# Mixing wide and narrow expert passes unit by unit in a two-block hybrid layer on one Trainium2 core

## The reference

```
def swiglu(x, w_gate, w_up, w_down):
    return (jax.nn.silu(x @ w_gate) * (x @ w_up)) @ w_down

def moe_swiglu(x, router_w, w_gate, w_up, w_down):
    logits = (x @ router_w).astype(jnp.float32)
    top_v, top_i = lax.top_k(logits, TOP_K)            # TOP_K = 2
    gates = jax.nn.softmax(top_v, axis=-1)
    combine = jnp.sum(jax.nn.one_hot(top_i, N_EXPERTS, dtype=jnp.float32) * gates[..., None], axis=-2)
    y = jnp.zeros_like(x)
    for e in range(N_EXPERTS):                         # 8 experts, inner width 3584
        y = y + combine[..., e:e + 1].astype(x.dtype) * swiglu(x, w_gate[e], w_up[e], w_down[e])
    return y
```

## Time and profile before

| | |
|---|---|
| median of three runs | 2535.86 us (2533.59 to 2536.7) |
| the profiled execution, its own time | 2543.58 us |
| its span | 2541.5 us |
| busy in the span: PE, DVE, ACT | 96%, 74%, 56% |
| HBM read | 589.79 MB, 232 GB/s over the span |
| expert passes written out, first split to last | 1590.4 to 2381.5 us of the span |
| the looped pass | 2393.1 to 2513.5 us |

### The profile page before, as it was taken

How to read it: one execution, slowest core, us unless ns; L and a number is a source line. 1 busy time by engine, 2 the same in 40 slices (tenths; PEclk the granted TensorE clock), 3 DMA queues, 4 the chain that set the end, 5 groups by cost and what they waited for, 6 DMA issues and landing times.

```text
span 2541.5 us, 36256 instructions
## 1 busy us (share of the span) xinstructions
PE 2433.5 (96%) x14462; PEld 2103.4 (83%) x14462; DVE 1880.7 (74%) x2198; ACT 1424.2 (56%) x1578; POOL 0.2 (0%) x4
## 2 busy tenths in 40 slices
PE   7999999999999999989999998999999999999897
PEld 7999989899998998886997885787777777888786
DVE  7665755567657543986554985889999999988787
ACT  4654444456545343423342422678888888777574
POOL 0000000000000000000000000000000000000000
PEclk9999999999999999999999998999999999999998
DMA  6333464343345444304534302899999999999796
GB/s 253 138 119 133 154 244 183 149 146 145 117 162 203 178 188 165 134 36 166 199 150 155 145 3 100 337 360 404 412 412 413 413 413 412 382 347 367 287 354 261
DMA packets 119623, 593.19 MB, mean 233 GB/s; under 512 B 17440, under 2 KB 17824, under 8 KB 77472
## 3 DMA queue, kind: packets, MB, share of 16 engines
q1 hardware_dynamic: 110224, 585.40, 59.8%
q10 hardware_dynamic: 9232, 5.47, 0.8%
HBM read 589.79 MB, written 1.05 MB: 232 GB/s over the span
## 4 chain that ended last, share of the span: by engine, by line
PE 69%; DVE 18%; DMA 5%; issue 4%; ACT 3%; DVEq 0%; SPq 0%; ACTq 0%; POOLq 0%
PE bank L608 21%; PE bank L2512 17%; PE bank L865 12%; DVE wlo L687 6%; DMA ring<-in_stream 5%; PE bank L1717 4%; DVE ring_lo L839 2%; ACT whi L682 2%; PE bank L1133 2%; DVE big L2967 1%; PE bank L1148 1%; PE bank L1738 1%; PE bank L1903 1%; PE bank L2452 1%; DVE big L2141 1%
## 5 line engine op out<-in xcount | busy, mean ns | idle before, releaser
L687 DVE TENSOR_TENSOR wlo<-ring,whi 128x2048 fp32r<-128x2048 f32 x430 | 979.0, 2289 | 113.0 <-ACT whi L682 108.8
L682 ACT ACTIVATE whi<-ring 128x2048 fp32r<-128x2048 f32 x433 | 825.9, 1912 | 111.6 <-PE bank L2512 51.4
L2512 PE MATMUL bank<-whi,xhi 128*128 128x512 f32 x896 | 367.7, 410 | 16.3 <-DVE wlo L687 12.5
L2512 PE MATMUL bank<-wlo,xhi 128*128 128x512 f32 x896 | 353.0, 394 | 0.0
L839 DVE TENSOR_TENSOR ring_lo<-ring,slot_hi 128x1024 fp32r<-128x1024 f32 x160 | 192.5, 1222 | 136.2 <-ACT slot_hi L816 125.9
L608 PE MATMUL bank<-xhi,whi 128*128 128x256 f32 x864 | 244.5, 283 | 2.4 <-DVE xlo L570 1.3
L608 PE MATMUL bank<-xhi,wlo 128*128 128x256 f32 x864 | 244.5, 283 | 0.0
L608 PE MATMUL bank<-xlo,whi 128*128 128x256 f32 x864 | 244.5, 283 | 0.0
L816 ACT ACTIVATE slot_hi<-ring 128x1024 fp32r<-128x1024 f32 x160 | 166.5, 1052 | 109.1 <-PE bank L865 79.1
L2512 PEld LDWEIGHTS bank<-whi,xhi 128*128 128x128 f32 x896 | 170.0, 190 | 64.8 <-DVE wlo L687 31.5
L865 PE MATMUL bank<-xh,slot_hi 128*128 128x256 f32 x704 | 203.1, 288 | 3.0 <-DVE ring_lo L839 3.0
(11 more groups left out here) (525 smaller groups left out, 4508.7 us busy)
## 6 DMA issues: line engine op xcount, KB each, us to landing
ring<-in_stream SPq DMA_DIRECT2D x555, 1024.0 KB, 7.2
par<-in_par ACTq DMA_DIRECT2D x2, 2048.0 KB, 9.1
con<-in_con SPq DMA_DIRECT2D x1, 1216.0 KB, 10.8
X<-in_x SPq DMA_DIRECT2D x2, 512.0 KB, 4.1
out_y<-X SPq DMA_DIRECT2D x2, 512.0 KB, 2.6
par<-in_par ACTq DMA_DIRECT2D x2, 448.0 KB, 6.0
par<-in_par ACTq DMA_DIRECT2D x2, 157.5 KB, 3.3
con<-in_con SPq DMA_DIRECT2D x1, 64.0 KB, 4.3
```

The costliest lines, as they stand in the source:

```text
L682: act.activation(whi[:, k % NSPLIT, :], src, ACT.Copy).then_inc(act_done, AC.step(tag + f".w{k}"))
L687: v.tensor_tensor(wlo[:, k % NSPLIT, :], src, whi[:, k % NSPLIT, :].bitcast(F32), ALU.subtract)\
L2512: mm = pe.matmul(out, left, right, start=start and i == 0, stop=stop and i == len(pairs) - 1)
```

## The change

- The 98 written-out units no longer run pass after pass. `TRACKS` puts the passes in a wide track (0, 5, 6, then the looped 7) and a narrow one (1, 2, 3, 4), and `straight_units` interleaves them by `STRETCHES`: (5 wide, 0 narrow), (9, 9), (4, 5), (5, 14), (5, 4), (7, 10), (7, 3), (0, 11), evenly within a stretch.
- The sum of a narrow pass lies in banks 6 and 7, that of a wide one in 4 and 5. All turns write bank 2 and wait for the unit before (`.hl` or `.h` of g-1, not of g-2). Bank 3, `aside`, takes all side work.
- `side_tasks` plans the side work, at most one task a unit, by earliest and latest unit: `put` (one a pass), `add` (four a pass, two matmuls and one DVE addition of 512 columns each), `gather` (two a pass, eight matmuls each). There are 45 tasks: 7 puts, 24 adds, 14 gathers. PE runs a task behind up1(g), after a wait for the reader of the task before. ACT and DVE empty the bank in the same row up1(g), ahead of their split of the slot three on.
- Narrow tokens lie in a tile of their own (`xn`). The one-hot matrices have four places; the copy `picked` (L2759) falls away in the written-out passes.
- Part 0 of the order of passes is computed in unit 0 and gives SP its table there; parts 1 and 2 move to units 5 and 7.
- The looped pass keeps its code apart from the one turn bank.

```diff
-WIDE_PASS = (0, 5, 6, 7)
+TRACKS = ((0, 5, 6, 7), (1, 2, 3, 4))
+WIDE_PASS = TRACKS[0]
+STRETCHES = ((5, 0), (9, 9), (4, 5), (5, 14), (5, 4), (7, 10), (7, 3), (0, 11))
...
+def straight_units():
+    per = DFF_EXP // 256
+    wide, narrow = ([(p, u) for p in track if p < NEXP - 1 for u in range(per)] for track in TRACKS)
+    units = []
+    for n_wide, n_narrow in STRETCHES:
+        one = [(wide.pop(0), (i + 0.5) / n_wide) for i in range(n_wide)]
+        one += [(narrow.pop(0), (i + 0.5) / n_narrow) for i in range(n_narrow)]
+        units += [unit for unit, _ in sorted(one, key=lambda y: y[1])]
+    return units
+
+def side_tasks(units):
...
+    waiting = {("put", ended[0], 0): (0, last[ended[0]])}
+    for j, p in enumerate(ended[:-1]):
+        for piece in range(4):
+            waiting[("add", p, piece)] = (last[p] + LAG + 1, last[ended[j + 1]] + LAG - 2)
+        waiting[("put", ended[j + 1], 0)] = (last[p] + LAG + 1, last[ended[j + 1]] + LAG)
+    for p in range(1, NEXP):
+        b = before[p]
+        start = 2 if b is None else first[b] + (6 if b == 0 else 2)
+        end = first[p] - 2 if p in first else len(units) - 4
+        for piece in range(2):
+            waiting[("gather", p, piece)] = (start, end)
...
             def turn(g):
-                if g >= 2:
-                    pe.wait_ge(vec_done, VE.at(tag + (f".hl{g - 2}" if is_wide(g - 2, rolled) else f".h{g - 2}")))
+                if g:
+                    pe.wait_ge(vec_done, VE.at(tag + (f".hl{g - 1}" if is_wide(g - 1, rolled) else f".h{g - 1}")))
...
+            def side(kind, p, piece):                                  # PE
+                for done, steps, name in aside_read[-1:]:
+                    pe.wait_ge(done, steps.at(tag + name))
...
+                elif kind == "add":
+                    t, cols = piece // 2, halves(piece % 2)
+                    pe.wait_ge(act_done, AC.at(tag + f".put{p}.0"))
+                    pe.wait_ge(vec_done, VE.at(tag + f"{p}.og"))
+                    pe.matmul(aside, put[:, t, :], og_hi[:, cols], start=True, stop=False)
+                    mm = pe.matmul(aside, put[:, t, :], og_lo[:, cols], start=False, stop=True)
+                    aside_read.append((vec_done, VE, name))
...
                 if kind == "up1" and g:                                 # ACT, and alike DVE
                     after_turn(g - 1)
...
+                if rolled is None and kind == "up1":
+                    for task, q, piece in tasks[g]:
+                        side(task, q, piece)
                 if k + LEAD < n:
                     a_split(act, tag, k + LEAD, rg_)
...
-                    if 1 <= u <= 3:
-                        v_order_passes(v, tag, u - 1)
...
+                    if g == 0:
+                        v_order_passes(v, tag, 0)
+                        take_seats(1)
+                    if g in (5, 7):
+                        v_order_passes(v, tag, (g - 3) // 2)
```

More of the change, by code:

```diff
@@ L96, in expert_order, with ready @@
     return order + [("down", g) for g in range(units - LAG, units)]
+def straight_units():
[8 more added lines that the diff above has]
+def side_tasks(units):
+    first, last = ({p: at(i for i, (q, _) in enumerate(units) if q == p) for p in range(NEXP - 1)} for at in (min, max))
+    ended = sorted(last, key=last.get)
+    track = {p: t for t in TRACKS for p in t}
+    before = {p: track[p][track[p].index(p) - 1] if track[p].index(p) else None for p in track}
+    tasks, at = {i: [] for i in range(len(units))}, {}
+    waiting = {("put", ended[0], 0): (0, last[ended[0]])}
[9 more added lines that the diff above has]
+            waiting[("gather", p, piece)] = (start, end)
+    def ready(key, i):
+        kind, p, piece = key
+        if i < waiting[key][0]:
+            return False
+        if kind == "put" and p != ended[0]:
+            return all(at.get(("add", ended[ended.index(p) - 1], q), i) < i for q in range(4))
+        if kind == "add":
+            return at.get(("put", p, 0), i) < i
+        if kind == "gather" and before[p] is not None and before[before[p]] is not None:
+            return at.get(("put", before[before[p]], 0), i) < i
+        return True
+    for i in range(len(units)):
+        can = sorted((k for k in waiting if ready(k, i)), key=lambda k: (waiting[k][1], k[2]))
+        if can:
+            key = can[0]
+            assert i <= waiting[key][1], (key, i, waiting[key])
+            tasks[i], at[key] = [key], i
+            del waiting[key]
+    assert not waiting, waiting
+    return tasks, at, ended, before
 def columns(spec):
@@ L328, in slot_index, with unit_of @@
             return up, dn
-        straight, over = expert_order(STRAIGHT * UNITS_EXP), expert_order(UNITS_EXP)
+        units = straight_units()
+        tasks, task_at, ended, before_in_track = side_tasks(units)
+        straight, over = expert_order(len(units)), expert_order(UNITS_EXP)
+        track_place = {p: track.index(p) for track in TRACKS for p in track}
+        def unit_of(g, rolled):
+            return units[g] if rolled is None else (0, g)
         def stream_slot(tag, k):
@@ L2503, in is_wide @@
         def is_wide(g, rolled):
-            return rolled is not None or g // UNITS_EXP in WIDE_PASS
+            return rolled is not None or units[g][0] in WIDE_PASS
+        aside = PS[3][:, :]
         def t_experts(pe, tag, order, rolled, ahead):
@@ L2661, in a_experts @@
                 at = tag + str(p)
-                if kind == "up0" and u == 8:
+                if rolled is not None and kind == "up0" and u == 8:
                     act.wait_ge(pe_done, PE.at(at + ".put"))
@@ new lines, in take_seats @@
+            def take_seats(p):
+                b = before_in_track[p]
+                if b is not None and before_in_track[b] is not None:
+                    v.wait_ge(pe_done, PE.at(tag + f".put{before_in_track[b]}.0"))
+                v_wait(v)
+                for t in range(NT):
+                    if p in WIDE_PASS:
+                        out, numbers = seats_of(p)[:, t, :], c("iota")
+                    else:
+                        out = seats_of(p)[:, t, :].rearrange("p (d c) -> p d c", d=2)
+                        numbers = c("iota")[:, 0:NARROW].unsqueeze(1).to_broadcast([P, 2, NARROW])
+                    v.tensor_scalar(out, numbers, place[:, t, p:p + 1], None, ALU.is_equal)\
+                     .then_inc(vec_done, VE.step(tag + f".seats{p}" if t else None))
@@ L2845, in v_experts @@
+                    if g == len(units) - 1:
+                        v.tensor_copy(ccol[:, 0:NT], wgt[:, :, ended[-1]]).then_inc(vec_done, VE.step())
+                if rolled is not None and kind == "up1":
+                    if u == 1:
+                        picks(at)
+                    if u in (4, 6):
+                        v_scatter(v, at, u // 2 - 2, wcol[:, u // 2 - 2:u // 2 - 1])
             if rolled is not None:
-                v_gather(v, tag + "0", rolled, True)
+                v_gather(v, tag + "0", rolled)
```

218 lines of the change are left out of this document (134 added, 84 removed).

## The result

The changed kernel takes 2542.19 us (median of 20 runs) beside 2536.64 us for the kernel before (20 runs): a ratio of 1.002, with a 95% interval of 1.0012 to 1.0028. It is slower by 3 to 7 us, and 21 us above the 2521 that were forecast. One of the 20 runs of the changed kernel took 3437.3 us at a mean granted clock of 0.65 and is left out of the ratio.

The account below looks back on a forecast made before the run. PE was taken to bound the wide windows and the fetch the narrow ones. Mixing them was to give -25.3 us and added waits +10, so -15 from 2535.9: a median of 2521 us, range 2507 to 2540.

Parts of the forecast that it names:

- Two regimes, the prices, the sums: PE bounds wide windows, fetch narrow ones; a wide unit costs PE 8.43 us, fetch 7.62; new stretches sum to 769.4 us.
- The added waits: Splits of slot k+3 wait behind puts and gather halves: 0.7 us for each of 14 events, 10 us.
- The free events: Of 21 puts and gathers, three in the opening and four in fetch-bound stretches were to cost nothing.
- Additions at nothing: Additions do not pass through ACT: 3.2 us of chain, under 3.8 in the worst case, so no added wait.
- The opening: Units 0-4: 50.0 us before, less 6.2 for parts 1 and 2, plus 4 for side work: 48.
- Parts 1 and 2 in units 5 and 7: Their 6.2 us of DVE work is paid in units 5-9, a stretch of 46.2 us set by DVE.
- One turn bank at nothing: turn(g) needs the readers of turn(g-1); in a narrow unit these had 1.8 us to spare, so no cost.
- Full carry: Rival: DVE's lead of up to three slots absorbs every event and the sums hold; -25, 2511 us; chance 0.17.
- No carry: Rival: the lead never passes from wide to narrow, each unit takes its own maximum; -4, 2532 us; chance 0.19.
- Mixing changes nothing: Rival: fetch slows when slots alternate between two experts, 2.5% more on 747 us; 2536 us; chance 0.03.
- Serialised side bank: Rival: with one bank for side work its emptying lies open on PE, 37 us; +22, 2558 us; chance 0.04.
- Lock-step: Rival: no carry, and DVE stands still at gather halves, 12 at 1.9 us; +19, 2555 us; chance 0.07.

Follow-up runs that it names:

- e3_empty_after: Changed kernel with ACT and DVE emptying the side bank behind their split of the slot three on: passes 764.3 us, 0.9903 of the kernel before.
- the last corner: Changed kernel with puts and gather halves emptied behind the split, additions still ahead: passes 767.9 us, 0.9902 of the kernel before.
- e8_all: Changed kernel with emptying behind the split, order-of-passes parts a row or two later, first put not before unit 4: passes 766.1 us, ratio 0.9903.
- e1_parts: Changed kernel with all three parts of the order of passes a row or two later on DVE: passes 791.5 us, 0.9988 of the kernel before.
- e7_unmixed_after: Changed kernel with the old order of units and all side work emptied behind the split: passes 791.3 us, 1.0007 of the kernel before.

## Why the prediction was wrong, point by point

**Two regimes, the prices, the sums: right.** With nothing late the passes take 764.3 us where the sums gave 769.4, and mixing is worth 27.0 us where the difference of the sums was 25.3. No stretch from unit 10 on is off by more than 3 us in e3_empty_after. The small error is the fetch price: stretches that the fetch was to set (10-22, 69-76, 87-97) came out 1.4 to 2.4 us shorter even in the changed kernel, 74.7 us instead of 76.2 for the last units. The ring holds up to six slots, and a stretch behind wide units probably starts with some of them fetched; no run tests that.

**The added waits: the step that failed.** It asked when the split of slot k+3 is needed *as a slot*, found 5.0 us of chain against PE's down(g-2), up0(g+1) and a turn, and took 0.7 us for each of 14 events, 10 us. Measured: 28.1 us for 21 puts and gather halves, 1.3 each, and 31.7 with the additions. Four things were wrong in it.

- *The deadline.* Behind the late split on DVE I had only splits queued ("Behind the waiting ACT and DVE only splits are queued"). That sentence is false for a wide unit: `gated` of the very unit stands one instruction behind, and the turn that needs it comes before slot k+3. For a wide unit the chain has another 0.41 us for the product (0.9 where seats come between, as at 2138.09), and PE has one turn less to fill it. The order of the changed kernel shows this: L755, then L2934. With this one step put right the prediction's own numbers give the gaps: 5.0 + 0.4 = 5.4 us of chain against 5.46 us of PE (two wide slots), 4.55 (one narrow) or 3.64 (two) is 0, 0.9 or 1.8 us, where 0.00, 0.71 to 1.06 and 1.61 to 1.97 were measured. It was only the turn that I had counted in, and the product that I had left out.
- *The lead comes back.* The bounds were 0 and 1.9 an event, and I went low since a wide unit returns DVE's lead. PE's turn doesn't draw on that lead: ACT waits for PE's own place in the program, so at each put and gather ACT's lead over PE is set to nil, however large it was, and DVE's with it. ACT's waits on L2764 and L2760 are 51 us in the passes over 14 gather halves, 17.8 over 7 puts.
- *The free events.* Three events in the opening and four in the stretches set by the fetch were priced at nothing. The opening lost 6.2 us by its three and units 32-50 lost 4.2 by theirs (two gather halves and a put), 2.1 and 1.4 us an event, no less than the mean of all: a stretch of 19 units is bound by the fetch on average, not at the wide unit that holds the gather (unit 37: 1.61 us).
- *The clock*, below: some 4 us of the 31.7 that no chain of instructions contains.

**Additions at nothing: right** to within 4 us, alone (+0.7) and in the last corner (3.6).

**The opening: wrong by 10.8 us**, the largest single miss, and half of it could be read. I took DVE's 6.2 us for parts 1 and 2 off a window that DVE did not set: the earlier trace rows have PE busy for 47.52 of its 50.00 us. Less DVE work could give back 2.5 at most, and the two gather halves and the put add 3.6 to PE. 47.5 + 3.6 is 51.1; e3_empty_after has 52.6 and e8_all 51.1. That the last two agree so well is in part luck, since 5.6 us of the 50.0 were at half clock. The other 6 us are the late turn 0: 3.1 of gap (5.30 for 2.16) and 2.7 of half clock behind it.

**Parts 1 and 2 in units 5 and 7: the price was right to 2 us** (46.2 for the stretch; 44.1 with the splits early, 51.3 as built). In the changed kernel they stand between a late split and a product, so they add to a wait that is already there: 4.15 us at turn 7, of which e1_parts got most back.

**One turn bank at nothing: right, as far as the runs tell.** No wait of a turn for the reads of the one before stands among the waits, and the old order with one turn bank and the emptying behind runs at 791.3 us against 790.6 with two, though that pair alone leaves room for some us, as said there. The Trainium skill (Perfetto Trace Analysis, Matmuls) would have matmul groups rotate through PSUM banks so that emptying overlaps; by its rule both single banks should have shown up as waits, and here they did not, because the reads were over before the next write was due. (The prediction calls what the rule would give "the last rival"; it is the fourth, the serialised side bank.)

**The wind-down: a little outside its bounds** of 1.5 either way: 9.9 us for 12.1 before by the same definition, 2.2 less, and 11.5 in e3_empty_after.

**The rivals.** Full carry (2511) is what the new order gives with nothing late: 2511.0 to 2514.5. No carry (worth 4 us) falls with the 27.0 of e7_unmixed_after. Mixing changes nothing falls with 411 GB/s in units 10 to 22. Serialised side bank: no side task waits for the reader of the one before; it falls, though half of the sign given for it, "waits of side matmuls or turns for DVE", is what came: the turns. A sign shared by two mechanisms was ascribed to one. Lock-step came nearest to the mechanism, by its description ("DVE stands still at each half of a gather") and by its price (12 halves at 1.9 are 23; the 14 halves were worth 17.3 alone), though it too looked at DVE's two splits and not at the product behind them. It was put on top of no carry and so given 2555 and a chance of 0.07. On top of the sums that hold, 769.4 + 23 is 792 of passes: 1.8 us more than before, 796.0 measured. Two independent questions (does the lead carry between kinds; is it lost at a side task) had been tied into one case.

Where the gain went, in one line: 791.3 - 764.3 = 27.0 us gained by mixing, 31.7 lost by emptying the bank ahead of the split, 0.7 for the rest: +5.4 in the passes.

## What to carry to other kernels

When an instruction is made to wait in an in-order queue, follow each instruction queued behind it to its own consumer, in program order, and take the earliest deadline among them; the tight one may be a 0.4 us step and not the big one. A copy-out that waits for work which the other engine has yet to do belongs behind the work that engine will need next, and an order that puts short rows among the long ones takes away the work that covered the wait (gaps of 0, 0.9 and 1.8 us with none, one and two narrow rows; 31.7 us for 15.2 in all), so the two must be costed together. Take time off a window only on the engine that its row shows as full.

## What the runs showed of the hardware

Long waits on PE were paid twice. After the 5.14 us at turn 0 the granted clock of TensorE was at half (the 1.2 GHz of its two levels) for 5.8 us, and again after the 3.99 us at turn 7 for 3.4 us. Windows of the changed kernel and PE's timeline there:

```profile
1594.20:1597.00 2.80, 2.72 (x8) 2.24 (x9) 2.56 (x3) 2.00 (x2) 0.00 (x0) 0.50 0.48 183
1597.00:1600.00 3.00, 3.00 (x9) 2.32 (x8) 2.29 (x1) 0.19 (x1) 0.00 (x0) 0.50 0.81 232
1600.00:1604.00 4.00, 4.00 (x20) 3.28 (x19) 2.01 (x2) 2.57 (x3) 0.00 (x0) 0.99 0.92 350
```
```profile
1664.98 0.66 PE L2614 MATMUL bank<-con,scr 128*128 128x128 f32 x2 [3.99 <-DVE scr L2934]
1665.29 0.78 PE L2590 MATMUL bank<-whi,xn 128*128 128x512 f32 x1
1665.86 0.63 PE L2590 MATMUL bank<-wlo,xn 128*128 128x512 f32 x1
...
1668.40 0.39 PE L2590 MATMUL bank<-wlo,xn 128*128 128x512 f32 x1
```

Matmuls of 512 columns followed each other every 0.43 us instead of 0.23, thirteen of them at turn 0 and seven at turn 7: 20 x 0.2 = 4 us. After the 1.81 us at 2139.04 the next ones are 0.23 apart again, and with the emptying behind the split, where the longest wait of a turn is 2.0 us, both windows are at full clock:

```profile
1582.30:1634.90 52.60, 49.00 (x237) 40.33 (x235) 44.83 (x70) 35.90 (x31) 0.00 (x0) 1.00 0.94 346
1634.90:1679.00 44.10, 43.24 (x233) 36.98 (x234) 41.61 (x46) 31.88 (x31) 0.00 (x0) 1.00 0.90 320
```

The opening of the kernel before had a granted clock of 0.94 too; I had not asked why, nor what a full clock there would be worth. Its trace has it at half for the first 2.2 us, from before the passes, and again for 3.4 us after a wait of 1.98 us at 1606.16. A third time, for 3.4 us, it was at half behind a wait of 2.10 us in a narrow pass:

```profile
1606.16 0.65 PE L2534 MATMUL bank<-con,scr 128*128 128x128 f32 x2 [1.98 <-DVE scr L2783]
```
```profile
1834.14 0.47 PE L2512 MATMUL bank<-whi,hhi 128*128 128x512 f32 x1 [2.10 <-DVE og_lo L2818]
```
```profile
1941.03 0.47 PE L2512 MATMUL bank<-whi,hhi 128*128 128x512 f32 x1 [2.12 <-DVE og_lo L2818]
```

The last line is the same wait one pass later, and the clock stayed full behind it. So the length of a wait alone does not settle it. Over the passes of all fourteen traces, the fourteen waits on PE of 1.76 to 1.93 us were each followed by full clock, all fifteen of 2.56 to 5.15 us by half clock for 3.4 or 6.8 us (counted in part before PE was back at work), and of the fourteen of 1.98 to 2.37 us two were and twelve were not. The changed kernel and the kernel before lost about the same by it in their profiled executions, some 4 to 5 us each.

The 31.7 us can be placed only roughly: gaps ahead of wide turns 24.2 - 6.9 = 17.3, half clock 4, waits for splits 26.3 - 14.6 = 11.7, 33 in all. That this is more than 31.7 is probably because some of these waits would have been spent on the fetch anyway; no run shows it.
